# A paged K cache loaded with four neighbouring rows per partition, and a block transposition that writes every fourth column

## The reference

```python
z = jnp.einsum("bqhd,bkhd->bhqk", q, k).astype(jnp.float32) * SB_SCALE + bias
log_om = jnp.where(mask, jax.nn.log_sigmoid(-z), 0.0)
suffix = lax.cumsum(log_om, axis=3, reverse=True) - log_om + carry[..., None]
a = jnp.where(mask, jnp.exp(jax.nn.log_sigmoid(z) + suffix), 0.0)
o = jnp.einsum("bhqk,bkhd->bqhd", a, v.astype(jnp.float32))
...
def page_step(state, phys):
    kp = cache_k[phys]
    vp = cache_v[phys]
```

## Time and profile before

| | us |
|---|---|
| median of 3 runs | 1264.17 |
| lowest and highest of them | 1261.17, 1271.37 |
| the profiled execution's own time | 1251.72 |
| its span in the profile | 1250.1 |

### The profile page before, as it was taken

The page is one execution under the profiler, slowest core; times in us unless marked ns, Lnnn a source line. Parts: engine busy times, 40 slices in busy tenths (PEclk is TensorE's granted clock), DMA queues, the critical chain, the costliest instruction groups (busy, mean ns, idle before and its releaser), DMA issues.

```text
span 1250.1 us, 22506 instructions
## 1 busy us (share of the span) xinstructions
PE 1039.0 (83%) x8241; PEld 880.3 (70%) x8241; DVE 690.7 (55%) x897; ACT 333.5 (27%) x560; POOL 415.1 (33%) x349
## 2 busy tenths in 40 slices
PE   5589988987457766548669887899999999999997
PEld 2267776755234444325459865899999999999996
DVE  0556856747456876657559644954455001554543
ACT  2432212132232433323241334422111121211121
POOL 0224544534221442235323101342423334342330
PEclk9789999989687888768789999999999999999998
DMA  9458999989997999999864112322221322322222
GB/s 348 137 162 236 294 273 283 286 217 298 294 323 205 267 293 281 282 263 293 249 208 167 34 69 101 101 84 86 67 92 50 102 92 70 99 68 74 63 63 76
DMA packets 125900, 220.48 MB, mean 176 GB/s; under 512 B 9951, under 2 KB 68580, under 8 KB 125812
## 3 DMA queue, kind: packets, MB, share of 16 engines
q1 hardware_dynamic: 101858, 144.01, 39.3%
q0 software_dynamic: 21120, 69.22, 19.4%
q10 hardware_dynamic: 2834, 6.13, 1.4%
HBM read 213.52 MB, written 5.80 MB: 175 GB/s over the span
## 4 chain that ended last, share of the span: by engine, by line
PE 56%; DMA 22%; DVE 10%; issue 5%; SPq 4%; ACT 2%; POOLq 1%; ACTq 0%; POOL 0%; DVEq 0%
PE ps L517 36%; DMA k_page<-in_cache_sb_k 15%; DMA v_early<-in_cache_sb_v 6%; PE ps L1593 5%; PE ps L578 4%; DVE kT L1329 3%; PE ps L1680 2%; PE ps L1549 2%; SPq L613 2%; PE ps L1724 1%; PE ps L361 1%; DVE h_lo L422 1%; SPq L636 1%; DVE r_sum L703 1%; SPq L622 1%
## 5 line engine op out<-in xcount | busy, mean ns | idle before, releaser
L473 POOL TENSOR_TENSOR w_lo<-w_raw,w_hi 128x2048 fp32r<-128x2048 f32 (+3 forms) x49 | 192.5, 3930 | 403.5 <-ACT w_hi L450 360.1
L1329 DVE STREAM_TRANSPOSE kT<-k_page 128x1024 f32<-128x1024 f32 x128 | 150.8, 1222 | 84.6 <-DMA k_page<-in_cache_sb_k 74.2
L517 PE MATMUL ps<-h_hi,w_hi 128*128 128x288 f32 x832 | 179.6, 297 | 11.5 <-DVE h_lo L422 8.4
L517 PE MATMUL ps<-h_lo,w_hi 128*128 128x288 f32 x832 | 178.6, 296 | 0.0
L517 PE MATMUL ps<-h_hi,w_lo 128*128 128x288 f32 x832 | 178.6, 296 | 0.0
L1680 PE MATMUL ps<-kT,q_bd 128*32 128x256 f32 x1024 | 89.1, 508 | 104.9 <-DVE kT L1329 104.8
L450 ACT ACTIVATE w_hi<-w_raw 128x2048 fp32r<-128x2048 f32 (+3 forms) x47 | 77.9, 1660 | 258.7 <-PE ps L517 227.2
L517 PEld LDWEIGHTS ps<-h_hi,w_hi 128*128 128x128 f32 x832 | 134.6, 189 | 12.7 <-issue 9.3
L1680 PEld LDWEIGHTS ps<-kT,q_bd 128*32 128x32 f32 x1024 | 37.4, 138 | 142.2 <-DVE kT L1329 110.5
L517 PEld LDWEIGHTS ps<-h_hi,w_lo 128*128 128x128 f32 x832 | 134.6, 189 | 0.0
L517 PEld LDWEIGHTS ps<-h_lo,w_hi 128*128 128x128 f32 x832 | 134.5, 189 | 0.0
(11 more groups left out here) (256 smaller groups left out, 1765.4 us busy)
## 6 DMA issues: line engine op xcount, KB each, us to landing
k_page<-in_cache_sb_k SPq DMA_DIRECT2D x128, 256.0 KB, 9.2
k_page<-in_cache_sb_k POOLq DMA_DIRECT2D x128, 256.0 KB, 8.2
v_late<-in_cache_sb_v SPq DMA_DIRECT2D x84, 256.0 KB, 7.6
v_late<-in_cache_sb_v POOLq DMA_DIRECT2D x84, 256.0 KB, 6.7
v_early<-in_cache_sb_v POOLq DMA_DIRECT2D x52, 256.0 KB, 7.1
mw_raw<-in_w_in SPq DMA_DIRECT2D x12, 1024.0 KB, 12.6
w_raw<-in_w_gate SPq DMA_DIRECT2D x11, 1024.0 KB, 5.2
w_raw<-in_w_up SPq DMA_DIRECT2D x11, 1024.0 KB, 5.3
```

The source lines that it names most:

```text
L473: return nc.gpsimd.tensor_tensor(w_lo[s][:, ks, :], w_raw[s][:, ks, :], w_hi[s][:, ks, :].bitcast(F32), ALU.subtract)
L517: op = nc.tensor.matmul(ps[:, 2 * t + hf, 0:b - a], weights[s][:, k, t * P:(t + 1) * P], x[:, k0 + k, a:b], start=begin and k == ks[0] and ...
L1329: nc.vector.transpose(slots[:, 4 * p + a:4 * p + a + 2, :, :], k_page[:, p, a:a + 2, :].rearrange("p a (b j) -> p a b j", j=32))\
```

## The change

Two expressions change. The load now gives partition `i` of a page's 32 the rows `4i` to `4i+3`, where it gave the rows `i`, `32+i`, `64+i` and `96+i`. The four rows are neighbours in the cache, 8 KB in one piece, and lie one behind the other on the partition as well. The transposition of the two rows `a`, `a+1` of every partition now writes key `4i + a` to column `128 p + 4i + a`, so the 32 numbers of a block's row go to every fourth column (16 bytes apart) instead of to 32 neighbouring ones. `kT` holds the same numbers at the same places as before, and everything that reads it is untouched. No wait, count or order of any instruction changes.

```diff
@@ -620,7 +620,7 @@
                 for g in gs:
                     page = page_of(eng, C, 4 * p + g)
                     eng.dma_start(k_page[32 * g:32 * g + 32, p, :, :],
-                                  ck[0, bass.ds(page, 1)].rearrange("o (a i) h d -> i (o a) (h d)", a=4))\
+                                  ck[0, bass.ds(page, 1)].rearrange("o (i a) h d -> i (o a) (h d)", a=4))\
                         .then_inc(s_kp[2 * p + g // 2], 16)
@@ -1319,14 +1319,14 @@
             def transposes(C):
-                slots = kT[:, :, :].rearrange("p b (x i) -> p x b i", i=32)
+                slots = kT[:, :, :].rearrange("p b (x i a) -> p x a b i", x=2, a=4)
                 for p in range(2):
                     dve.wait_ge(s_kp[2 * p], 32 * (C + 1))
                     dve.wait_ge(s_kp[2 * p + 1], 32 * (C + 1))
                     if p == 0 and C:
                         dve.wait_ge(m_["score"], (PER + 1) * ((C - 1) // PER) + (C - 1) % PER + 2)
                     for a in (0, 2):
-                        nc.vector.transpose(slots[:, 4 * p + a:4 * p + a + 2, :, :],
+                        nc.vector.transpose(slots[:, p, a:a + 2, :, :],
                                             k_page[:, p, a:a + 2, :].rearrange("p a (b j) -> p a b j", j=32))\
                             .then_inc(s_ktr, 1)
```

## The result

| | before | changed |
|---|---|---|
| median, us | 1258.34 (8 runs) | 1273.45 (8 runs) |
| lowest and highest | 1253.0, 1271.37 | 1269.26, 1279.12 |
| the profiled execution's span | 1250.1 | 1277.4 |

The ratio is 1.0112, with a 95% interval of 1.0069 to 1.0155: the change costs 15 us where 16 were forecast as a gain.

The account below looks back on a forecast made before the run. The prediction took the first half to be bound by DMA transfers, K loads above all, and the second by PE. Its terms, -11 - 5 + 0 = -16 us, took 1264 to 1248 us, range 1222 to 1298.

Parts of the forecast that it names:

- What bounds the kernel: First step: the first half is bound by transfers, its loop runs at the DMA engines' pace, K costing 1.45 times V.
- K load, longer pieces: K load in the chunk loop: one 8 KB run per partition instead of four of 2 KB, claimed to save 11 us.
- The 8.6%: K load: saving per KB of 4 and 6 KB rows over V's 2 KB rows, taken as 5.5 ns per KB for K.
- first rival: K load: nothing changes because a page's 32 partitions bind; only balance might give something, 1262 us; chance 0.25.
- The rival with long packets: K load: long packets hold neighbouring engines together, K stays at 216 GB/s, 81 ns per KB; 1299 us, chance 0.15.
- Balance of the two queues: K loads on SP's and POOL's queues: with 8 KB runs on both, the two land together, claimed to save 5 us.
- Transposition: DVE transpositions writing every fourth column: claimed to cost nothing more, staying at 1.2 us each, so 0 us.
- The rule that spoke against the edit: Transposition: the Trainium skill's SBUF lines of 16 bytes, needing at least two hits per line, would make it slower.
- The rival's price of 1.0 us: Transposition: writes in steps cost +1.0 us each, taken as +50 us in all, 1298 us; chance 0.15.
- Sum: Whole kernel: -11 - 5 + 0 = -16 us, from 1264 us to a forecast of 1248 us.
- The stated range: Whole kernel's time: 1222 to 1298 us, leaving out together 0.2 of the chance.

Follow-up runs that it names:

- e6: Kernel before, with each K page loaded to all 128 partitions in 2 KB rows, the sample's attention left out of what is computed; ratio to before 0.9384.
- e10: Kernel before, with each K page loaded to 32 partitions four apart instead of 32 neighbouring ones, the sample's attention left out; ratio to before 0.9437.
- e1: Kernel before with the change's load alone (8 KB pieces) and the old transposition, the order of the keys left out; ratio to before 1.0055.
- e11: e10 with the change's load (four neighbouring rows, one 8 KB piece per partition), the sample's attention left out; ratio to before 0.9369.
- e5: e1 with k_page laid out so that the neighbouring rows load in 2 KB pieces, the order of the keys left out; ratio to before 0.9981.
- e3: e1 with the order of the keys put right by the scores' matmul reading kT in steps of 32 numbers, all computed; ratio to before 1.0077.
- e2: Kernel before with the change's transposition alone (every fourth column) and the old load, the order of the keys wrong; ratio to before 1.0060.

## Why the prediction was wrong

*What bounds the kernel.* Right. The loss is in the chunk loop alone, and the loop hangs on K's rate: e6 and e10, which raise it, take 6% off.

*K load, longer pieces: forecast -11 us, measured +7* (e1, 0.55% of 1261). This is the step that failed first. The 8.6% was read from rows of loads that go to all 128 partitions and carried over to one that goes to 32. The prediction's own rows said that these are different regimes (81 ns per KB while one side of the partitions is written), and its first rival said what follows: the ports bind. The term should have been nothing, with the gain only where e11 has it: K was to fall from 64 to 58.5 ns per KB, and takes 68 to 69 in e1, where the packets of 8 KB are K's alone. That it is even a loss was in no rival in this form. The rival with long packets had the right sign and named the length of the piece, but K didn't drop to its 216 GB/s or 81 ns. Whether the loss comes of K's slightly dearer bytes or of landings that lie further apart stays open.

*Balance of the two queues: forecast -5; no gain from it shows.* The row that it was read from, 585 to 588 us, lies in what the prediction itself calls a V phase, and evenness was taken for time. Issue to landing of K, SP's and then POOL's, is 9.2 and 8.2 us before and 9.4 and 8.1 in e5 (short pieces), 9.6 and 8.7 in e1 and 9.0 and 8.8 in e3 (long ones). The two do come nearer, but mostly since POOL's loads take longer. The even 7.5 and 7.7 of the changed kernel go with its slow transposition, as e2 shows.

*Transposition: forecast 0, measured +0.78 us on each and +7.5 us in all* (e2, 0.60% of 1261). This step failed as well. The value was taken from L1380, a copy of 32 numbers, since its median was that of L1458. At 0.76 ns per number, 32 numbers would show 24 ns, and L1380's own durations run from 142 to 252: it could not tell. The rule that spoke against the edit was set aside on its account. The rival's price of 1.0 us was nearer. But its end, +50 us, was far too much: 128 x 0.78 = 100 us of DVE work came through as 7.5, one part in thirteen. Part of the work lies where DVE had waited for K: that wait fell from 74 us to 29 in e2. And the DMA engines hardly stood idle for it: the two queues hold 95.5% of them from 95 to 600 us in e2, for 97.6% before. What covers the rest was not taken apart; the loop had more cover than one dense window of 31 us made it seem.

*Sum.* Forecast -16, measured +15: +7 and +7.5 in place of -16 and 0. The stated range, 1222 to 1298, holds the time, but by its width; its weight lay on the other side.

## What to carry to other kernels

A cost per byte that is read from one load holds for another only if both write the same part of the partitions. Look first whether a load's rate is half of the others' when it is alone; if so, work on where it lands, since longer pieces bought nothing here, and those of 8 KB lost time. A block transposition on DVE could write its float32 results to every second place for nothing, but not to every fourth. A price per number has to be read from rows long enough to show it. When a stage's queue times shrink after a change, ask whether the loads became faster or were only issued later: a kernel with the other half of the change alone tells.

## What had not been expected of the hardware

- The transposition's price is a step, not a slope: 1203, 1206, 1984 and 2028 ns for writes 4, 8, 16 and 32 bytes apart.
- A matmul that reads its 256 float32 columns 128 bytes apart takes at least 608 ns, for 379 with columns that lie together (e3).
- Pieces of 8 KB in place of 2 KB made the kernel 0.55% slower where 32 neighbouring partitions are written, and 0.7% faster where they lie four apart (e1, and e11 against e10).
- Which 32 partitions a page goes to is worth 5.6% of the whole kernel (e10). No way was tried to use this with all computed: as the kernel is built, the 32x32 transpositions need each page's keys on 32 neighbouring partitions.
